# Expert weights loaded as four neighbouring rows per partition, with every fourth feature as the matching operand

## What is computed

```python
def expert_choice_ffn(h, w_router, w_gate, w_up, w_down):
    b_, t_, d_ = h.shape
    cap = CAPACITY_FACTOR * t_ // N_EXPERTS
    aff = jax.nn.softmax(jnp.einsum("btd,de->bte", h, w_router).astype(jnp.float32), axis=-1)
    top_aff, top_idx = lax.top_k(jnp.swapaxes(aff, 1, 2), cap)
    xin = jax.vmap(lambda hb, ib: hb[ib])(h, top_idx)
    g = jnp.einsum("becd,edf->becf", xin, w_gate)
    u = jnp.einsum("becd,edf->becf", xin, w_up)
    y = jnp.einsum("becf,efd->becd", jax.nn.silu(g) * u, w_down) * top_aff[..., None].astype(h.dtype)
    return jax.vmap(lambda yb, ib: jnp.zeros((t_, d_), h.dtype).at[ib.reshape(-1)].add(yb.reshape(-1, d_)))(y, top_idx)
```

## Time and profile before

| | us |
|---|---|
| median of 3 runs | 1255.58 (1250.82 to 1259.35) |
| the profiled execution | 1254.22 |
| its span, first to last instruction | 1252.4 |

### The profile page before, as it was taken

How to read it: one execution, slowest core, us unless ns; L and a number is a source line. 1 busy time by engine, 2 the same in 40 slices (tenths; PEclk the granted TensorE clock), 3 DMA queues, 4 the chain that set the end, 5 groups by cost and what they waited for, 6 DMA issues and landing times.

```text
span 1252.4 us, 11145 instructions
## 1 busy us (share of the span) xinstructions
PE 977.6 (78%) x4368; PEld 483.6 (39%) x4368; DVE 420.1 (34%) x643; ACT 208.9 (17%) x426; POOL 48.2 (4%) x101
## 2 busy tenths in 40 slices
PE   4799989998887777566666666666665998998987
PEld 2666456654443442111111111111112764544843
DVE  1398244616741342111111111111224264411422
ACT  2123132312441211000000000000002033301010
POOL 0100000001010100000000000000001000000000
PEclk9899989998898878877777777777777999998999
DMA  9934253844639507999999999999997441023000
GB/s 355 330 134 167 102 201 133 304 153 150 231 133 391 211 1 283 410 409 410 410 409 410 410 410 410 409 410 410 409 410 289 155 152 68 1 85 117 1 1 33
DMA packets 102230, 310.44 MB, mean 248 GB/s; under 512 B 2705, under 2 KB 4932, under 8 KB 102068
## 3 DMA queue, kind: packets, MB, share of 16 engines
q1 hardware_dynamic: 99700, 301.04, 62.4%
q0 software_dynamic: 2496, 8.93, 2.0%
HBM read 308.91 MB, written 1.05 MB: 247 GB/s over the span
## 4 chain that ended last, share of the span: by engine, by line
PE 57%; DMA 29%; DVE 7%; SPq 2%; issue 2%; ACT 1%; POOL 1%; POOLq 0%; ACTq 0%; DVEq 0%
PE bank L760 39%; DMA ring<-w_up_dram 27%; PE bank L1091 7%; PE bank L778 3%; DMA ring<-w_ada_dram 2%; SPq L659 1%; PE bank L768 1%; PE bank L889 1%; PE bank L1107 1%; PE bank L788 1%; PE bank L974 1%; SPq L644 1%; PE bank L1196 1%; DVE state L2045 1%; PE bank L1219 1%
## 5 line engine op out<-in xcount | busy, mean ns | idle before, releaser
L1091 PE MATMUL bank<-ring,ilat 128*32 128x512 f32 x1024 | 140.4, 699 | 48.2 <-DMA ring<-w_up_dram 48.2
L1107 PE MATMUL bank<-ring,ilat 128*32 128x512 f32 x512 | 95.7, 915 | 11.7 <-ACT ilat L1507 11.7
L760 PE MATMUL bank<-ring,hT 128*128 128x512 f32 x224 | 101.9, 616 | 3.7 <-DVE gates L1850 2.0
L760 PE MATMUL bank<-ring,kT 128*128 128x512 f32 (+1 forms) x224 | 97.8, 598 | 5.2 <-DVE kT L1616 3.4
L2043 DVE TENSOR_SCALAR state<-state 64x512 f32<-64x512 f32 x16 | 6.7, 419 | 256.9 <-ACT state L1505 256.9
L1091 PEld LDWEIGHTS bank<-ring,ilat 128*32 128x32 f32 x1024 | 35.3, 124 | 149.0 <-issue 92.1
L1098 PE MATMUL bank<-const,state 128*128 128x128 f32 x64 | 17.9, 434 | 95.7 <-DVE state L2049 95.7
L760 PE MATMUL bank<-hT,ring 128*128 128x256 f32 (+1 forms) x320 | 86.4, 431 | 3.6 <-DVE hT L1654 3.6
L760 PEld LDWEIGHTS bank<-hT,ring 128*128 128x128 f32 x320 | 61.6, 194 | 28.3 <-issue 17.7
L1119 PE MATMUL bank<-state,ilat 128*128 128x512 f32 x128 | 58.7, 602 | 14.6 <-DVE state L2051 14.6
L760 PEld LDWEIGHTS bank<-ring,hT 128*128 128x128 f32 x224 | 43.9, 198 | 59.2 <-issue 57.3
(11 more groups left out here) (319 smaller groups left out, 1096.3 us busy)
## 6 DMA issues: line engine op xcount, KB each, us to landing
ring<-w_down_dram SPq DMA_DIRECT2D x32, 2048.0 KB, 19.9
ring<-w_gate_dram SPq DMA_DIRECT2D x32, 2048.0 KB, 18.9
ring<-w_up_dram SPq DMA_DIRECT2D x32, 2048.0 KB, 23.0
ring<-w_ada_dram SPq DMA_DIRECT2D x24, 2048.0 KB, 11.6
ring<-w_in_dram SPq DMA_DIRECT2D x8, 2048.0 KB, 13.3
ring<-fno_w_in_dram SPq DMA_DIRECT2D x4, 2048.0 KB, 8.8
ring<-w_out_dram SPq DMA_DIRECT2D x2, 2048.0 KB, 15.5
ring<-mla_w_in_dram SPq DMA_DIRECT2D x2, 2048.0 KB, 21.8
```

The lines of the kernel that those rows point to most:

```text
L760: ins = pe.matmul(o, l, r, start=start and i == 0, stop=stop and i == len(terms) - 1)
L1091: ins = pe.matmul(bank[0][32 * t:32 * t + 32, :], xin_cur[:, j, :], w[2 * half + t // 2][:, j % JH, n0:n0 + TN], start=j == 0, stop=j == J ...
L1107: ins = pe.matmul(bank[2 + n][32 * q:32 * q + 32, :], hmT[:, q, 32 * c:32 * c + 32], w[4 + c][:, q, n * TN:(n + 1) * TN], start=c == 0, st ...
```

## The change

A tile of the experts' weights now gives partition p the rows 4p to 4p + 3 of the half, which lie together in HBM as one piece of 16 KB, instead of four rows that stand 128 apart. The destination is the slot as one flat row per partition. Block j of a slot then holds rows 4p + j, so everything that meets it takes every fourth feature: a step of 4 elements (16 bytes) in the stationary operand of the transposes L768 of this stage and L1098, of the `xin` products and of `mod_columns` for modulation tiles 6 to 9; the router's weights come in pieces of four rows; the norm row and the bias rows are permuted on the host. The number and order of matmuls, copies and waits stay as they are.

```diff
+def spread(x):
+    return x.rearrange("p (h q j) -> p h j q", q=P, j=4)
...
+FFN_MODS = [6, 7, 8, 9]
...
         def expert_src(w, e, half):
-            return w[bass.ds(e, 1), half * TN:(half + 1) * TN, :].rearrange("e (j p) n -> p (e j) n", p=P)
+            return w[bass.ds(e, 1), half * TN:(half + 1) * TN, :].rearrange("e (p j) n -> p (e j n)", p=P)
...
+        def expert_slot(s):
+            return ring[:, s * SLOT:(s + 1) * SLOT]
...
-                    sp.dma_start(expert_view(s), expert_src(w, e, half)).then_inc(landed[s], 16)
+                    sp.dma_start(expert_slot(s), expert_src(w, e, half)).then_inc(landed[s], 16)
...
-            pool.dma_start(router, a["w_router"][0].rearrange("(j p) e -> p j e", p=P)).then_inc(sem("router_in"), 16)
+            pool.dma_start(router4, a["w_router"][0].rearrange("(h p j) e -> p h j e", p=P, j=4)).then_inc(sem("router_in"), 16)
...
-                    ins = pe.transpose(o[:, jj * P:(jj + 1) * P], src[:, j * P:(j + 1) * P], ident)
+                    chunk = spread(src)[:, g, jj, :] if interleaved else src[:, j * P:(j + 1) * P]
+                    ins = pe.transpose(o[:, jj * P:(jj + 1) * P], chunk, ident)
...
-                    ins = pe.matmul(o[:, 2 * jj:2 * jj + 2], x[:, jj * P:(jj + 1) * P], C("sum_columns"),
+                    chunk = spread(x)[:, 0, jj, :] if i in FFN_MODS else x[:, jj * P:(jj + 1) * P]
+                    ins = pe.matmul(o[:, 2 * jj:2 * jj + 2], chunk, C("sum_columns"),
...
-                fills(sum_of(o[:, :], [(xn[:, b, j * P:(j + 1) * P], onehot2[:, b, :]) for b in range(TB)]),
+                fills(sum_of(o[:, :], [(spread(xn[:, b, :])[:, j // 4, j % 4, :], onehot2[:, b, :]) for b in range(TB)]),
...
-                    ins = pe.transpose(bank[1][:, k * P:(k + 1) * P], hidden_rows[:, k * P:(k + 1) * P], ident)
+                    ins = pe.transpose(bank[1][:, k * P:(k + 1) * P], spread(hidden_rows)[:, 0, k, :], ident)
```

More of the change, by code:

```diff
@@ L560, in block_program @@
         router = qh[:, 0:J * E].rearrange("p (j e) -> p j e", j=J)
+        router4 = qh[:, 0:J * E].rearrange("p (h j e) -> p h j e", h=2, j=4)
         logit = smat[:, 0:TB * E].rearrange("p (b e) -> p b e", b=TB)
@@ L653, in _ @@
                 w, half = expert_tiles[s]
-                sp.dma_start(expert_view(s), expert_src(w, 0, half)).then_inc(landed[s], 16)
+                sp.dma_start(expert_slot(s), expert_src(w, 0, half)).then_inc(landed[s], 16)
             with sp.Fori(1, E) as e:
@@ L761, in sum_of, with turn_chunks @@
                 return ins
-            def turn_chunks(name, src, g):
+            def turn_chunks(name, src, g, interleaved=False):
                 o = pe_take(pe, name)
@@ L1036, in _ @@
                 for g in range(2):
-                    turn_chunks(("x1T", b, g), xn[:, b, :], g)
+                    turn_chunks(("x1T", b, g), xn[:, b, :], g, True)
             for b in range(TB):
@@ L2185, in laid_out, with interleaved @@
     arrays = {n: np.ascontiguousarray(inputs[n]) for n in _DIRECT}
-    arrays["rows"] = np.concatenate([np.asarray(inputs[_ROW_SOURCES[n]]).reshape(-1, P) for n in ROWS])
+    def interleaved(x):
+        return np.asarray(x).reshape(-1, P, 4).transpose(0, 2, 1).reshape(-1, P)
+    arrays["rows"] = np.concatenate([interleaved(inputs[_ROW_SOURCES[n]]) if n == "pre_ffn"
+                                     else np.asarray(inputs[_ROW_SOURCES[n]]).reshape(-1, P) for n in ROWS])
     arrays["bias_rows"] = np.concatenate([np.asarray(inputs[n]).reshape(-1, P) for n in ("b_ada", "b_ada_2")])
+    ffn = slice(4 * FFN_MODS[0], 4 * FFN_MODS[-1] + 4)
+    arrays["bias_rows"][ffn] = interleaved(arrays["bias_rows"][ffn])
     arrays["const"], arrays["mask"], arrays["fft"] = CONST, level_masks(), fourier_constants()
```

## The result

| us | before | after |
|---|---|---|
| median | 1254.62 (4 runs, 1250.82 to 1259.35) | 1235.97 (4 runs, 1234.31 to 1239.02) |
| ratio, 95% interval | | 0.9852 [0.9811, 0.9893] |
| profiled execution, its span | 1254.22, 1252.4 | 1234.52, 1232.7 |

The change takes off 1.5%. The forecast was 1236 us. The changed kernel was run twice more beside the experiments: 0.9852 [0.9826, 0.9877] and 0.9861 [0.9841, 0.9881].

The account below looks back on a forecast made before the run. DMA transfer of expert weights was taken to bound the loop. From 1254.22 us, 19.4 came off for 88 shorter tiles and 1.0 was added for stepped loads: 1235.8, given as 1236, range 1228 to 1248.

Parts of the forecast that it names:

- What bounds: Expert loop: DMA transfer sets the period of 30.73 us, with 3.3 us to spare on TensorE's side.
- The cost of a packet: Expert tile loads: 75.4 ns per 2 KB plus fixed 9.2 ns; 16 KB takes 612.4 ns, a tile 4.90 us against 5.12.
- The number of tiles: Expert loop: 88 tiles lie on the path, each 0.22 us shorter, so 19.4 us come off.
- Does TensorE keep up: Expert loop: period 29.4 us against TensorE's chain of 27.43; the up tile wait shrinks from 3.3 to about 2.0 us.
- SyncE's issue: SyncE's queue: up tiles issue sooner than 4.11 us, but nothing waits for them, so nothing is gained.
- The stepped loads: TensorE weight loads with a 16-byte step, in loop, router, xin and modulation: cost 0 to 10.6 us, taken as 1 us.
- the main term: Expert loop: the 19.4 us saved by loading tiles in 16 KB pieces instead of 4 KB.
- A smaller gain per packet: Expert tiles: half of the fixed 9.2 ns may hang on bytes or each 4 KB; about 1246 us, within a 0.11 case.
- no effect: Expert tiles: 16 KB still moved as four 4 KB packets, tiles stay at 5.12 us; 1254 to 1257 us, chance 0.10.
- slow long packets: Expert tiles: 16 KB packets take 0.87 us each, 162 us more, 1416; chance 0.09 shared with the other slower mechanism.
- the doubled loads are all paid: Stepped weight loads: the full doubling is paid, giving back about 10 us; 1246 us, within a 0.11 case.
- the stepped transposes bind the loop: L1098 loads: bind from 0.49 us more each; at 0.83 more, 1267 us; chance 0.09 shared with the other slower mechanism.

Follow-up runs that it names:

- a_again: The changed kernel run once more, with no edit, beside the kernel before: 1235.32 us, ratio 0.9852 [0.9826, 0.9877].
- one_4k: Changed kernel, but each expert tile comes in one DMA in the old layout (4 KB pieces), stepped operand reads kept: 1256.55 us, ratio 1.0013 to the kernel before.

## Why the prediction was right, and where not

**What bounds.** Right. TensorE waits for the up tile in both traces, and with half the bytes the loop fell to another bound.

**The cost of a packet.** Right in all its parts: 612.4 ns forecast, 612.0 measured, 4.90 us a tile. The stretch of 6 KB pieces in the earlier trace rows was a weak support, too short to tell 418 from 422; the pieces of 8 KB and 2 KB in the same loop are the strong one. The Trainium skill's rule of about 3 cycles a packet (DMA: Bandwidth & Descriptors, "Why small descriptors are slow (HBM only)") asked for 1.7% less time. The loop's period fell by 4.4%, from 30.73 to 29.38 us. The measurement decides.

**The number of tiles.** 88 x 0.22 = 19.4 us, measured 19.57 from first issue to last release.

**Does TensorE keep up.** Right in the outcome, wrong in a size. The wait was to shrink from 3.3 to 2.0 us in each expert. It was between 1.9 and 4.1 us, changing from expert to expert, 2.9 on average. The chain of 27.43 us was not a constant: where the products of tiles 2 and 3 got the full clock they took 3.64 us, not 5.34, and the chain was 905.12 + 3.64 - 883.19 = 25.57. A chain read from a trace in which the engine waits holds the clock that the waiting left it.

**SyncE's issue.** Right: 4.11 to 0.37 us, worth nothing.

**The stepped loads.** The term was 1.0 us; measured as a whole 1.6 [-0.1, 3.3]. The single parts were off. The step that failed is the argument for the value near the lower end, that a load at its usual length isn't at the limit of what SBUF can give. At full clock a load without the step is fast enough for the step to show: those of `mod_columns` became 1.7 times as long, 0.192 to 0.330 us, for 32 loads 4.4 us, of 6.1 allowed, and their stage 3.5 us longer. At the lower clock the load takes 0.333 us with or without the step. The prediction priced the transposes by the loads of 0.226 us in the earlier trace rows, which are those at the lower clock; nothing changed there, of 0.9 allowed in the loop. Of the router's sixteen, for which 3.6 us were allowed, the eight at full clock went from 0.140 to 0.210 us. The xin loads were covered as forecast (their products went from 16.1 to 16.4 us). The Trainium skill's penalty for reads where each element lies in another 16-byte line (Advanced Engine Details and Errata, "Memory Cachelines") is thus seen in this case, with 0.138 us a load of `mod_columns`, but at full clock alone. And the trace after happened to hide the price: with `a_again`'s clock from tile 12 to the loop its profiled time would have been 3.5 us more. That the median of four runs, 1235.97, meets the forecast of 1236 so closely is therefore partly luck; the size of the main term is not.

**The rivals.** A smaller gain per packet, no effect and slow long packets are excluded by the table of pieces; that the doubled loads are all paid, by the 3.3 us that `one_4k` leaves at most; and that the stepped transposes bind the loop, by their 0.224 us. The packets of 0.87 us in the earlier trace rows were told about instruction fetches alone; 16 KB of weights took 0.61.

## What to carry to other kernels

Where a stretch is bound by DMA at an even rate, compute the time of one piece at two lengths from the trace and draw the line: the fixed part tells what longer pieces are worth (here 9.4 ns a piece, 5.9% from 2 to 4 KB, 3.0% to 8 KB, 1.5% more to 16 KB). A layout that gives each partition neighbouring rows cost nothing in the load, and its price lies in the other operand. ScalarE's copy took the permutation without getting longer; so did weight loads at the lower clock, and those beside long matmuls. Loads at full clock that nothing covers are the place to keep it out of, though here that gained nothing that could be measured in the whole time. Read a load's price at the clock at which it runs. Count the tiles between the first issue and the last release, since only those pay.

## What the runs showed of the hardware that I had not expected

- A weight load of 128 x 128 float32 with a step of 16 bytes is longer than one with step 1 only at full clock: 0.330 against 0.192 us for a matmul and 0.210 against 0.140 for a transpose at a granted clock of 1.00, but 0.329 against 0.333 and 0.226 against 0.231 at 0.50. ScalarE's copy from PSUM with the same step takes the same 0.597 us as without.
- The issue of a 2 MB DMA with 512 pieces occupies SyncE for up to 5.0 us while the queue is full (4.4 in the median for the up tiles of 500 to 930 us, 0.6 for the gate tiles), and for 0.33 to 0.38 us with 128 pieces.
- Two DMAs of 1 MB in place of one of 2 MB leave the rate of a full queue as it was. The first 10 us after an empty queue ran at 271 GB/s with two DMAs of 4 KB pieces and at 326 with one, in one trace each.
- The granted clock in one stretch of 35 matmuls was 1.00 in one run and 0.62 in another of the same kernel, 3.5 us apart, as much as the stepped loads add to their stage.
